# Offsets between the matmul operands in SBUF: the high parts 32 bytes off the weights' line, modulo 512

## The chip, the cores and the metric

The program runs on 1 core of one Trainium2 chip. The metric is the device time of one execution in microseconds (us). Most executions of one kernel agree within 0.3%. A second figure is the span of a profiled execution, from the first to the last instruction in the trace.

## The reference

Two transformer blocks run one after the other on 512 tokens of width 1024, all in float32. What matters here is where the matrix products are:

```python
def first_block(x, ...):
    h = x
    h = h + hybrid_mixer(rms_norm(h, norm1_g), w_in, ..., w_out)
    h = h + sq_relu_mlp(rms_norm(h, norm2_g), w_up, w_down)
    return rms_norm(h, final_norm_g)

def second_block(x, c, ...):
    h = rmsnorm(x, g_norm1) * (1.0 + scale1) + shift1
    proj = h @ w_in
    ...
    merged = (jax.nn.sigmoid(gate_fox) * (y_fox @ w_branch_fox)
              + jax.nn.sigmoid(gate_dsa) * (y_dsa @ w_branch_dsa))
    x = x + gate1 * (merged @ w_out)
    h2 = rmsnorm(x, g_norm2) * (1.0 + scale2) + shift2
    x = x + gate2 * (jnp.square(jax.nn.relu(h2 @ w_mlp1)) @ w_mlp2)
    return rmsnorm(x, g_final)
```

The mixers (a gated convolution and a chunked retention in the first block; forgetting attention and a top-128 sparse attention in the second) stand between the projections. Each MLP has an inner width of 4096.

## The kernel before

**Three products for one.** Every large product is made in fp32r from operands that are split in two. Weights come from HBM into `raw` (512 KB a piece, one of four slots). ScalarE copies a slot to `w_hi` (line 1213), which rounds it, and GpSimd writes the rest, `w_lo = raw - w_hi` (line 542). The activations are split the same way: `u_hi`/`u_lo` hold the output of a norm, `y_hi`/`y_lo` the inner activations of an MLP or the outputs of the attention heads, `m_hi`/`m_lo` the merged branches ahead of the second `w_out`. A product is then the sum of high by high, high by low and low by high, gathered in one PSUM bank.

**The loop that does most of the work** is `unit` (line 581): for each of 8 chunks of the contraction it issues three matmuls of 128x512. The tensor named first in the call is the stationary one (the 128x128 block that is loaded into the array), the second is the moving one (128x512, streamed through):

```python
for k in ks[part[0]:part[1]]:
    c = slice(k * P, k * P + cols)
    for w, r in ((w_hi, r_hi), (w_hi, r_lo), (w_lo, r_hi)):
        last = pe.matmul(ps[0:cols, bank, :], w[:, s, c], r[:, k, :], ...)
```

`r` is `u` in the norm-fed products and the first half of each MLP, `y` in the second half of the first MLP, `m` in the second block's `w_out`. In the profile a matmul is written `ps<-moving,stationary`, so `ps<-u_hi,w_hi` streams `u_hi` past `w_hi`. In some places the roles are turned: `rv_pass` (line 727) and `value_slot` (1008) hold `u` and stream the weights, `down_rows` (1127) and `last_down_rows` (1157) hold `y` and stream the weights in the order (y_hi, w_hi), (y_hi, w_lo), (y_lo, w_hi). `branch` (1071) holds weights and streams `y`.

**The order of the work** is written out by hand in each engine's block; semaphores `raw_ready`, `hi_ready`, `lo_ready`, `used` and `bank_free` hand the four weight slots and the PSUM banks around. While the array streams for one matmul, the stationary block of the next is loaded. Attention work (lines 960 to 987) is laid between pieces of `unit` from about 670 to 840 us.

**Addresses.** A helper `sb(name, shape, dtype)` places tensors one behind the other in each partition; each starts at the next multiple of 32 bytes, and a stack (`where=`) lets later tensors take the place of closed ones. `sb("to_line", [P, 72])` fills up to address 32768, where `xres` starts. From there on `xres`, `u_hi`, `u_lo`, `y_hi`, `y_lo` and `raw`, `w_hi`, `w_lo` follow with 16 KB each, a multiple of 512 bytes, so all of them start at 0 modulo 512. So do `m_hi`, `m_lo`, `q_up`, `q_dn`, `k_both` and `vtoks`, which lie behind them. A chunk of an activation is 2048 bytes wide and a 128-column block of weights 512 bytes, so that every operand of the matmuls above starts at 0 modulo 512.

Of the kernel before, what the change touches and what calls it, by code (L numbers as in the profile page):

```python
# [25 lines left out]
F32R = mybir.dt.float32r  # L26
# [4 lines left out]
P = 128  # L31
T = 512
NT = T // P
D = 1024
KC = D // P
# [9 lines left out]
SLOTS = 4  # L45
# [126 lines left out]
def build(nc, tab, x, norm1_g, w_in, conv_w, conv_norm_g, ret_norm_g, w_out, norm2_g, w_up, w_down,  # L172
# [30 lines left out]
    with ctx:  # L203
        def sb(name, shape, dt=F32, where=ctx):
            return where.enter_context(nc.sbuf_tensor(name, shape, dt))
# [31 lines left out]
        sb("to_line", [P, 72])  # L237

        xres = sb("xres", [P, KC, T])
        u_hi, u_lo = sb("u_hi", [P, KC, T], F32R), sb("u_lo", [P, KC, T], F32R)  # L240
        y_hi = sb("y_hi", [P, KC, T], F32R)
        scores = ExitStack()
        sb("y_lo_front", [P, NQ, T], where=scores)
        work = sb("work", [P, NT - 1, T], where=scores)
# [1 line left out]
        scores.close()  # L246
        y_lo = sb("y_lo", [P, KC, T], F32R)
        raw = sb("raw", [P, SLOTS, KC * P])
        w_hi, w_lo = sb("w_hi", [P, SLOTS, KC * P], F32R), sb("w_lo", [P, SLOTS, KC * P], F32R)

        one = ExitStack()
        fades = sb("fades", [P, P + 4 * NQ], where=one)
# [30 lines left out]
        two = ExitStack()  # L283
        merge = ExitStack()
        vtoks = sb("vtoks", [P, 2, NT, QW], where=merge)
        q_up, q_dn = sb("q_up", [P, 4, T], F32R, where=merge), sb("q_dn", [P, 4, T], F32R, where=merge)
        merge.close()
        m_hi, m_lo = sb("m_hi", [P, KC, T], F32R, where=two), sb("m_lo", [P, KC, T], F32R, where=two)
        keys_done = ExitStack()
        gates = sb("gates", [P, 4, T], where=keys_done)  # L290
        keys_done.close()
# [2169 lines left out]
```

## Time and profile before

| | |
|---|---|
| median of 3 runs | 1351.55 us (1351.45 to 1351.58) |
| the profiled execution's own time | 1352.54 us |
| its span | 1350.7 us |
| PE (matmul) busy | 1339.7 us, 99% of the span |
| weight loads (PEld) busy | 1094.2 us |
| DVE, ACT, POOL busy | 756.1, 525.9, 563.0 us |
| mean granted TensorE clock | 0.998 |

The profiled execution took 1.0 us more than the median of the runs, of which 1.8 us lie outside its span. In the profile a matmul's duration is longer than its share of the array: it begins when its turn starts and its modelled end lies behind the last column's way through the array, so neighbours overlap. What a matmul costs in a stream is the distance from its start to the next start.

### The profile page before, as it was taken

The numbers are of one execution on the slowest core, as the hardware profiler recorded it, in microseconds if no ns is written. First come the engines' busy times: TensorE is split into PE (matmuls) and PEld (weight loads), VectorE is DVE, ScalarE is ACT, GpSimd is POOL, SyncE is SP. The second block draws the span as 40 slices with busy tenths as digits, with TensorE's granted clock in tenths as the row PEclk, the third lists the DMA queues.
The fourth block names the chain that finished last, engine by engine and source line by source line (L and its number), as shares of the span: only waits on it lengthen the run. The fifth ranks groups of instructions, "written<-read, shape, count | busy, mean of one in ns | idle before, by whom it ended". The sixth has DMA issues, their size and how long they took to land.

```text
span 1350.7 us, 18066 instructions
## 1 busy us (share of the span) xinstructions
PE 1339.7 (99%) x6376; PEld 1094.2 (81%) x6380; DVE 756.1 (56%) x1085; ACT 525.9 (39%) x830; POOL 563.0 (42%) x230
## 2 busy tenths in 40 slices
PE   9999999999999999999999999999999999999998
PEld 8888878888888888886877777888878888888887
DVE  4555578475664655877788774434563241432355
ACT  6344234422323224254366665232355133142333
POOL 5334344454553635524222223444434534345351
PEclk9999999999999999999999999999999999999999
DMA  7232245555655645423212323333423423324221
GB/s 230 80 97 78 91 130 171 164 167 177 198 168 163 183 143 166 112 91 95 63 56 86 95 63 94 109 94 105 129 73 100 125 78 109 93 79 123 78 94 63
DMA packets 212807, 155.74 MB, mean 115 GB/s; under 512 B 8932, under 2 KB 193760, under 8 KB 212744
## 3 DMA queue, kind: packets, MB, share of 16 engines
q1 hardware_dynamic: 212280, 154.43, 38.4%
q8 instruction: 39, 0.64, 0.2%
q10 hardware_dynamic: 464, 0.48, 0.1%
q14 instruction: 24, 0.20, 0.0%
HBM read 152.75 MB, written 4.74 MB: 117 GB/s over the span
## 4 chain that ended last, share of the span: by engine, by line
PE 53%; DVE 1%; ACT 1%; issue 0%; POOL 0%; ACTq 0%; DVEq 0%
PE ps L581 28%; PE ps L1127 11%; PE ps L1071 3%; PE ps L1008 3%; PE ps L987 1%; PE ps L974 1%; PE ps L1157 1%; PE ps L960 1%; PE ps L961 1%; PE ps L947 0%; PE ps L964 0%; PE ps L921 0%; PE ps L925 0%; PE ps L922 0%; PE ps L1096 0%
## 5 line engine op out<-in xcount | busy, mean ns | idle before, releaser
L542 POOL TENSOR_TENSOR w_lo<-raw,w_hi 128x1024 fp32r<-128x1024 f32 x222 | 560.0, 2530 | 758.1 <-ACT w_hi L1213 738.0
L581 PE MATMUL ps<-u_hi,w_hi 128*128 128x512 f32 x944 | 378.5, 401 | 0.8 <-POOL w_lo L542 0.5
L581 PE MATMUL ps<-u_hi,w_lo 128*128 128x512 f32 x944 | 368.3, 390 | 0.0
L581 PE MATMUL ps<-u_lo,w_hi 128*128 128x512 f32 x944 | 367.5, 389 | 0.0
L1213 ACT ACTIVATE w_hi<-raw 128x1024 fp32r<-128x1024 f32 x222 | 231.6, 1053 | 289.3 <-PE ps L581 116.8
L581 PEld LDWEIGHTS ps<-u_hi,w_lo 128*128 128x128 f32 x944 | 177.2, 188 | 37.7
L581 PEld LDWEIGHTS ps<-u_hi,w_hi 128*128 128x128 f32 x944 | 178.1, 189 | 36.3 <-issue 1.6
L581 PEld LDWEIGHTS ps<-u_lo,w_hi 128*128 128x128 f32 x944 | 177.6, 188 | 34.9 <-issue 1.0
L581 PE MATMUL ps<-y_hi,w_hi 128*128 128x512 f32 x320 | 125.3, 391 | 0.1
L581 PE MATMUL ps<-y_hi,w_lo 128*128 128x512 f32 x320 | 124.5, 389 | 0.0
L581 PE MATMUL ps<-y_lo,w_hi 128*128 128x512 f32 x320 | 124.5, 389 | 0.0
L1432 ACT ACTIVATE nsq<-ps 128x512 f32<-128x512 f32 x64 | 38.3, 598 | 198.6 <-PE ps L581 193.6
L1127 PE MATMUL ps<-w_hi,y_hi 128*128 128x512 f32 x224 | 87.1, 389 | 0.0
L1127 PE MATMUL ps<-w_lo,y_hi 128*128 128x512 f32 x224 | 87.1, 389 | 0.0
L1127 PE MATMUL ps<-w_hi,y_lo 128*128 128x512 f32 x224 | 87.1, 389 | 0.0
L2000 DVE SCALAR_TENSOR_TENSOR acc<-adaw,vec,acc 128x1536 f32<-128x1536 f32 x28 | 82.5, 2946 | 1.9 <-DVE y_lo L2054 1.5
L2110 DVE TENSOR_TENSOR nt<-nsq 128x512 f32<-128x512 f32 x32 | 27.9, 873 | 98.1 <-ACT nsq L1432 98.0
L2049 DVE TENSOR_TENSOR nt<-nsq 128x512 f32<-128x512 f32 x32 | 24.3, 758 | 84.5 <-ACT nsq L1432 83.9
L581 PEld LDWEIGHTS ps<-y_hi,w_hi 128*128 128x128 f32 x320 | 60.1, 188 | 13.9 <-issue 1.1
L581 PEld LDWEIGHTS ps<-y_lo,w_hi 128*128 128x128 f32 x320 | 60.1, 188 | 12.5 <-issue 0.2
L581 PEld LDWEIGHTS ps<-y_hi,w_lo 128*128 128x128 f32 x320 | 60.1, 188 | 12.6
L2132 DVE SCALAR_TENSOR_TENSOR nt<-ps,rinv,gate_row 128x512 f32<-128x512 f32 x21 | 15.8, 751 | 92.4 <-PE ps L1127 92.4
(317 smaller groups left out, 1878.8 us busy)
## 6 DMA issues: line engine op xcount, KB each, us to landing
raw<-w_in SPq DMA_DIRECT2D x69, 512.0 KB, 3.7
raw<-w_mlp SPq DMA_DIRECT2D x64, 512.0 KB, 3.8
adaw<-w_ada SPq DMA_DIRECT2D x32, 768.0 KB, 4.6
raw<-w_up SPq DMA_DIRECT2D x32, 512.0 KB, 6.1
raw<-w_down SPq DMA_DIRECT2D x32, 512.0 KB, 5.5
raw<-w_out SPq DMA_DIRECT2D x16, 512.0 KB, 4.2
bias_rows<-bias_rows SPq DMA_DIRECT2D x4, 635.0 KB
xtok<-x SPq DMA_DIRECT2D x4, 512.0 KB, 7.3
```

The lines of the kernel that those rows point to most:

```text
L542: pool.tensor_tensor(w_lo[:, s, :], raw[:, s, :], w_hi[:, s, :], ALU.subtract).then_inc(lo_ready[s], 1)
L581: last = pe.matmul(ps[0:cols, bank, :], w[:, s, c], r[:, k, :], start=(k == ks[0] and w is w_hi and r is r_hi), stop=(k == ks[-1] and w is ...
L960: pe.matmul(ps[:, bank, 0:keys], q_up[:, at, q], k_both[:, at, 0:keys], start=True, stop=False)
L1008: last = pe.matmul(ps[:, i, :], u[:, k, t], w[:, s, c], start=(k == 0 and u is u_hi and w is w_hi), stop=(k == KC - 1 and u is u_lo))
L1071: last = pe.matmul(ps[:, b, :], w[:, 2, c], r[:, k, :], start=(k == k0 and w is w_hi and r is y_hi), stop=(k == k0 + NQ - 1 and w is w_lo))
L1127: last = pe.matmul(ps[:, i, :], h[:, k, t], w[:, s, c], start=(k == 0 and h is y_hi and w is w_hi), stop=(k == KC - 1 and h is y_lo))
L1213: act.activation(w_hi[:, s, :], raw[:, s, :], ACT.Copy).then_inc(hi_ready[s], 1)
L1432: act.activation(nsq[:, s % 2, :], ps[:, s, :], ACT.Relu).then_inc(bank_free[s], 1)
L2000: dve.scalar_tensor_tensor(a, adaw[:, b, :], c, a, ALU.mult, ALU.add).then_inc(sem("acc_done"), 1)
L2049: dve.tensor_tensor(nt[:, s % 2, :], nsq[:, s % 2, :], nsq[:, s % 2, :], ALU.mult).then_inc(sem("mlp_sq"), 1)
L2110: dve.tensor_tensor(nt[:, s % 2, :], nsq[:, s % 2, :], nsq[:, s % 2, :], ALU.mult).then_inc(sem("mlp_sq"), 1)
L2132: dve.scalar_tensor_tensor(gated[i], ps[:, i, :], facts[:, i:i + 1], gate_row[:, c], ALU.mult, ALU.mult).then_inc(bank_free[i], 1)
```

## The change

Small fillers are put between the tensors, and three declarations of two tensors are split so that a filler can stand between them. Nothing else is touched: no instruction is added or removed, and the order on every engine stays.

```diff
         xres = sb("xres", [P, KC, T])
-        u_hi, u_lo = sb("u_hi", [P, KC, T], F32R), sb("u_lo", [P, KC, T], F32R)
+        sb("to_line1", [P, 4])
+        u_hi = sb("u_hi", [P, KC, T], F32R)
+        sb("to_line2", [P, 4])
+        u_lo = sb("u_lo", [P, KC, T], F32R)
+        sb("to_line3", [P, 4])
         y_hi = sb("y_hi", [P, KC, T], F32R)
+        sb("to_line4", [P, 118])
...
         raw = sb("raw", [P, SLOTS, KC * P])
-        w_hi, w_lo = sb("w_hi", [P, SLOTS, KC * P], F32R), sb("w_lo", [P, SLOTS, KC * P], F32R)
+        sb("to_line5", [P, 126])
+        w_hi = sb("w_hi", [P, SLOTS, KC * P], F32R)
+        w_lo = sb("w_lo", [P, SLOTS, KC * P], F32R)
+        sb("to_line7", [P, 60])
...
         vtoks = sb("vtoks", [P, 2, NT, QW], where=merge)
+        sb("to_line_q", [P, 8], where=merge)
         q_up, q_dn = sb("q_up", [P, 4, T], F32R, where=merge), sb("q_dn", [P, 4, T], F32R, where=merge)
         merge.close()
-        m_hi, m_lo = sb("m_hi", [P, KC, T], F32R, where=two), sb("m_lo", [P, KC, T], F32R, where=two)
+        m_hi = sb("m_hi", [P, KC, T], F32R, where=two)
+        sb("to_line_m", [P, 8], where=two)
+        m_lo = sb("m_lo", [P, KC, T], F32R, where=two)
```

With every start rounded up to 32 bytes, a filler of 4 numbers (16 bytes) takes 32 bytes, one of 118 takes 480, one of 126 takes 512, one of 60 takes 256 and one of 8 takes 32. The starts modulo 512 become:

| tensor | before | after | after, from `w_hi` |
|---|---|---|---|
| xres | 0 | 0 | -64 |
| u_hi | 0 | 32 | -32 |
| u_lo, y_lo, raw, w_hi, w_lo | 0 | 64 | 0 |
| y_hi | 0 | 96 | +32 |
| m_hi, vtoks | 0 | 320 | +256 |
| m_lo, q_up, q_dn, k_both, probt_even, prob_odds | 0 | 352 | +288 |

`nt`, `nsq`, `small` (the identity), `ones`, `prob_evens` and `probt_odd` lie ahead of `xres` and stay at 128.

## Rows read from the trace of the kernel before

**Rows 1.** The page's head: span, and busy time, share and instructions of PE.

```profile
span 1350.7 us, 18066 instructions
...
PE 1339.7 (99%) x6376; PEld 1094.2 (81%) x6380; DVE 756.1 (56%) x1085; ACT 525.9 (39%) x830; POOL 563.0 (42%) x230
```

**Rows 2.** Who made PE wait: us in total, times, longest us (longest row).

```profile
PE ps L644 <- POOL epsc L537: 1.4, 1, 1.4
```

**Rows 3.** The chain that ended last: start us, us, what, with its count.

```profile
947.02 43.53 PE ps L581 x192
...
1323.21 13.62 PE ps L1157 x60
```

**Rows 4.** Matmul groups of the split products, shapes apart: count | busy us, mean ns.

```profile
L581 PE MATMUL ps<-u_hi,w_hi 128*128 128x512 f32 x944 | 378.5, 401 | 0.8 <-POOL w_lo L542 0.5 <-issue 0.2
...
L581 PE MATMUL ps<-y_hi,w_hi 128*128 128x512 f32 x320 | 125.3, 391 | 0.1
...
L1127 PE MATMUL ps<-w_hi,y_hi 128*128 128x512 f32 x224 | 87.1, 389 | 0.0
...
L1008 PE MATMUL ps<-w_hi,u_hi 128*128 128x512 f32 x64 | 26.4, 413 | 0.0
...
L1071 PE MATMUL ps<-y_hi,w_hi 128*128 128x512 f32 x64 | 24.9, 389 | 0.0
...
L581 PE MATMUL ps<-m_hi,w_hi 128*128 128x512 f32 x64 | 24.9, 389 | 0.0
...
L727 PE MATMUL ps<-w_hi,u_hi 128*128 128x512 f32 x32 | 12.3, 400 | 0.5 <-issue 0.5
...
L1157 PE MATMUL ps<-w_hi,y_hi 128*128 128x512 f32 x28 | 10.9, 389 | 0.0
```

**Rows 5.** Timeline of PE in the first MLP, first and twelfth matmul in a row.

```profile
259.82 0.39 PE L581 MATMUL ps<-u_hi,w_hi 128*128 128x512 f32 x1
...
262.31 0.39 PE L581 MATMUL ps<-u_hi,w_lo 128*128 128x512 f32 x1
```

**Rows 6.** Timeline of the weight loads at the same place.

```profile
260.05 0.19 PEld L581 LDWEIGHTS ps<-u_hi,w_lo 128*128 128x128 f32 x1
260.27 0.19 PEld L581 LDWEIGHTS ps<-u_hi,w_hi 128*128 128x128 f32 x1
```

**Rows 7.** Timeline of PE at the end, 256 columns moving: first and last of 24.

```profile
1342.09 0.28 PE L1157 MATMUL ps<-w_hi,y_hi 128*128 128x256 f32 x1
...
1344.84 0.28 PE L1157 MATMUL ps<-w_hi,y_lo 128*128 128x256 f32 x1
```

**Rows 8.** Window around 620 us: us, busy of five engines, granted clock, DMA share, GB/s.

```profile
619.00:621.50 2.50, 2.50 (x7) 1.92 (x7) 2.31 (x7) 0.64 (x1) 1.78 (x1) 0.50 0.00 0
```

**Rows 9.** Timeline of PE in that window, first and sixth matmul in a row.

```profile
619.13 0.63 PE L1008 MATMUL ps<-w_hi,u_hi 128*128 128x512 f32 x1
...
621.27 0.63 PE L1008 MATMUL ps<-w_hi,u_lo 128*128 128x512 f32 x1
```

**Rows 10.** Timeline of PE after a run of transposes, nine starts in a row (five shown).

```profile
68.14 0.39 PE L581 MATMUL ps<-u_lo,w_hi 128*128 128x512 f32 x1
68.38 0.39 PE L581 MATMUL ps<-u_hi,w_lo 128*128 128x512 f32 x1
...
69.08 0.39 PE L581 MATMUL ps<-u_hi,w_lo 128*128 128x512 f32 x1
69.30 0.39 PE L581 MATMUL ps<-u_hi,w_hi 128*128 128x512 f32 x1
...
70.00 0.38 PE L674 MATMUL ps<-qf,kf 128*128 128x128 f32 x2
```

**Rows 11.** The weight slots' makers, GpSimd and ScalarE, and one DMA issue line.

```profile
L542 POOL TENSOR_TENSOR w_lo<-raw,w_hi 128x1024 fp32r<-128x1024 f32 x222 | 560.0, 2530 | 758.1 <-ACT w_hi L1213 738.0
...
L1213 ACT ACTIVATE w_hi<-raw 128x1024 fp32r<-128x1024 f32 x222 | 231.6, 1053 | 289.3 <-PE ps L581 116.8
...
raw<-w_mlp SPq DMA_DIRECT2D x64, 512.0 KB, 3.8
```

**Rows 12.** Window over the attention stretch, columns as in rows 8.

```profile
640.00:840.00 200.00, 198.66 (x1229) 156.78 (x1233) 149.06 (x404) 116.60 (x257) 54.72 (x23) 1.00 0.29 79
```

## The prediction

> **What bounds the kernel now.** I read the page's head first. PE is busy for 1339.7 of 1350.7 us [rows 1], and the longest of its few waits is 1.4 us [rows 2]: no engine and no DMA holds PE up, so only the length of PE's own stream counts. The mean durations of the groups (389 to 413 ns) [rows 4] are no price, because neighbours overlap. The price is the distance between starts, and the chain of waits gives it best: 192 matmuls of 128x512 in 43.53 us, which is 226.7 ns each [rows 3]. The timeline says the same, 11 distances in 2.49 us, 226.4 ns [rows 5].
>
> At full clock (2.4 GHz) 512 columns at one per cycle would take 213.3 ns. So each of these matmuls carries 13.3 ns, or 32 cycles, that stream nothing. Three views say what kind of thing this is:
> - With 256 columns moving, 23 distances take 2.75 us, 119.6 ns each [rows 7]; 256 columns are 106.7 ns, so the extra is 12.9 ns. It belongs to a matmul (or to its weight load), not to a column.
> - At half clock (granted 0.50, that is 1.2 GHz) [rows 8], five distances take 2.14 us, 428 ns [rows 9]; 512 columns are 426.7 ns. Here the extra is gone. A fixed number of TensorE cycles for changing weights would have shown as 27 ns each, 133 ns over the five. So the extra looks like data that don't come fast enough at full clock, not like work of the array.
> - The load of the next stationary block starts with the stream of the current matmul: loads at 260.05 and 260.27, matmuls every 0.227 from 259.82 [rows 5, 6]. Two reads of SBUF run at once, both from a start at 0 modulo 512.
> - Right behind a run of transposes the same matmuls with the same addresses are uneven: 8 distances in 1.86 us, 232.5 ns in the mean, with steps of 0.24 us (68.14 to 68.38) and of 0.22 us (69.08 to 69.30) [rows 10]. Only their phase in time is different. A toll that each weight load pays in any case would not do this.
>
> I read this as two SBUF reads that get into each other's way by a measure that depends on how they lie to each other. An offset in address is then as good as one in time, and this is what the change touches.
>
> **The change part by part.** It removes and adds no instruction, DMA or wait. Three things move.
>
> (1) What streams against what is loaded. In a triple of `unit` with `u`, the pairs (moving now, loaded for the next) are (u_hi, w_hi), (u_lo, w_lo), (u_hi, next w_hi). After the change their distances modulo 512 are -32, 0, -32 bytes; with `y` moving +32, 0, +32; with `y` held and weights moving (lines 1127, 1157) -32, 0, -32; with `m` 256, 288, 256. So of each triple two are shifted, and all three for `m`. The groups of [rows 4] hold 944 + 320 + 224 + 64 + 64 + 64 + 32 + 28 = 1740 triples, 5220 matmuls. Shifted are 2 x 1676 + 3 x 64 = 3544 of them.
>
> The trace of before has no 128x512 fp32r matmul with a shifted pair, so the price of one is bounded from both sides. Best end: the whole extra goes, 213.3 ns, -13.3 ns each, 3544 x 13.3 = -47.3 us. Worst end: each costs the longest step seen, 0.24 us [rows 10], +13.3 ns, +47.3 us. The nearest row is the one in which only the phase differs [rows 10]. It shows a step of 0.22 us (0.215 to 0.225 at its two decimals) as its shortest, and 232.5 ns as its mean. I take 222 ns, the upper half of the shortest step, because the third matmul of a triple stays as it was and hands its state on to the next. That is -4.67 ns each, 3544 x 4.67 = **-16.5 us**.
>
> A rule speaks against this. The Trainium skill ("SBUF — State Buffer", section on the two separate sides) says that PE never waits on another reader. By it the distance to the loaded block could do nothing and this sum would be zero; the uneven distances and the half-clock row [rows 9, 10] do not fit it well, though it speaks of other engines and not of PE's own two reads. The same skill ("TensorE: Matmul & The Clock Gate", back-to-back issue gap) gives N/2.4 + 2.5 ns, 215.8 ns for 512 columns, so by that page the extra here is 10.9 ns, and an estimate with all of it gone from the shifted ones is -38.5 us; the trace shows 226.7, not 215.8.
>
> (2) The splitters. ScalarE, GpSimd and DVE now read and write tensors at other offsets. `raw`, `w_hi`, `w_lo` keep their distance of 0, so the 2530 and 1053 ns a slot [rows 11] stand. The splits of activations now have 32 bytes between their two sides. Priced at zero: a slot is used by 24 matmuls, 5.44 us, against 2.53 us of GpSimd and 1.05 us of ScalarE, and DMA pieces land 3.8 us after issue [rows 11], with four slots in turn. Even at the best end, 5.12 us a slot, this cover holds. The cover would be gone only with GpSimd at twice its time; then every slot would cost PE what GpSimd takes beyond 5.1 us.
>
> (3) Attention operands. `k_both` and `q` stay at one distance (+288 both), `vtoks` and `probt_even` get 32 bytes apart, and the identity stays at 128 while `prob_odds` goes to 352. These are 128-column pieces among 1229 matmuls in 200 us [rows 12]. I take zero, with +/-1 us for the range. In this stretch DVE is busy 149 of 200 us and PE idle 1.3; DVE is what is late next if PE gets quicker there, and it may keep 1 or 2 us of the gain.
>
> Sum: 1350.7 - 16.5 = 1334.2 us of span, 1336.0 us for an execution like the profiled one (1352.54), and, as its own time stands 1.0 us over the median of the runs, **1335.0 us** against 1351.55.
>
> **The rivals.**
> - A, the forecast: shifted pairs get in each other's way less, but not never. 1335 us; from 1346 (1.5 ns each) to 1317.
> - B, full relief: the shifted pairs run at 213.3 to 216 ns, 3544 x 10.7 to 13.3 = -38 to -47 us, 1304 to 1313 us. For it: the extra is wholly absent at half clock [rows 9]. Against: 0.22 us is the shortest step that any phase has brought [rows 10].
> - C, nothing: the extra is a toll of any weight load at full clock, whatever the addresses (one port taken in turns). 1351.5 us. For it: it is the same 12.9 to 13.3 ns in the steady rows of lines 581 and 1157 [rows 3, 7]. Against: the uneven steps. To this belongs that the change doesn't do what it says, if a filler of 16 bytes were not rounded to 32; the starts listed ahead speak against it.
> - D, slower: the even 226.7 ns is a settled state, which the stream finds when every pair has the same distance. With -32, 0, -32 each matmul hands the next a changed phase and the stream never settles; every shifted matmul then costs the unsettled mean of 232.5 ns [rows 10], +5.8 ns, 3544 x 5.8 = +20.6 us, 1372 us. It decides as soon as the mean of a triple passes 226.7 ns. For it: all unsettled phases but one in [rows 10] cost more than the settled one. Against: the unsettled steps are on both sides of 226.7, so the settled state is not the best.
>
> **How the numbers follow.** A measurement of this kernel can tell about 0.2%, 2.7 us. Chances: A 0.37, B 0.14, C 0.18, D 0.31. So faster 0.51, same 0.18, slower 0.31. The time is that of A, the likeliest. For the range I leave out the lower half of B and the end of D: 1309 to 1371 us. A alone would be 1317 to 1346.
>
> **What would show it.** In the changed kernel the chain's row of 192 matmuls (43.53 us) should read about 42.9 us where `u` or `y` is in play (two of three at 222), and the starts in the first MLP should step by 0.22, 0.23, 0.22. B would give 41.8 us and steps of 0.21 or 0.22; C exactly 43.5; D 44.2 or more, with uneven steps in the MLPs where there are none now. The `m` product tells 256 and 288 apart from 32: if its row changes and the others don't, the distance matters but 32 bytes are too few. Weight loads should keep their 0.19 us and their start with the stream. I am wrong in kind if the steady rows stay at 226.7 ns, or if the time changes through waits on `w_lo`, or in the attention stretch alone.

## The result, and the profile after

The changed kernel takes 1378.01 us (1377.91 to 1379.37, 3 runs) against 1351.55 us, a ratio of 1.0199 (95% interval 1.0176 to 1.0222). It is slower by 26.5 us; 1335 us were forecast, and the range ended at 1371. The spans of the two profiled executions differ by 26.9 us.

The head of the page after, answering to [rows 1]:

```profile
span 1377.6 us, 18066 instructions
...
PE 1366.7 (99%) x6376; PEld 1094.2 (79%) x6380; DVE 757.8 (55%) x1085; ACT 526.1 (38%) x830; POOL 562.6 (41%) x230
```

The chain of waits after (start us, us, what, with its count), answering to [rows 3]. Lines are 11 further on than before: 592, 1138 and 1082 for 581, 1127 and 1071.

```profile
952.75 5.58 PE ps L592 x24
958.33 5.55 PE ps L1082 x24
963.88 44.80 PE ps L592 x192
...
1059.39 44.53 PE ps L1138 x192
1103.91 44.80 PE ps L592 x192
```

PE still works all the time, with the same instructions and the same 1094.2 us of weight loads. Each matmul of 512 columns is only further from the next. What stood at 43.52 us for 192 is now 44.80 where `u` or `m` is streamed (233.3 ns each) and 44.53 where `y` is held (231.9 ns); where `y` is streamed (line 1082) 24 take 5.55 us (231.2 ns), where 24 at the old price are 43.53 / 8 = 5.44 us. The timeline of PE in the first MLP, which was even before [rows 5], shows how (start us, us, engine, line, operation):

```profile
264.84 0.40 PE L592 MATMUL ps<-u_hi,w_lo 128*128 128x512 f32 x1
265.07 0.40 PE L592 MATMUL ps<-u_hi,w_hi 128*128 128x512 f32 x1
265.31 0.39 PE L592 MATMUL ps<-u_lo,w_hi 128*128 128x512 f32 x1
265.54 0.40 PE L592 MATMUL ps<-u_hi,w_lo 128*128 128x512 f32 x1
...
267.64 0.40 PE L592 MATMUL ps<-u_hi,w_lo 128*128 128x512 f32 x1
```

12 distances from 264.84 to 267.64 take 2.80 us, 233.3 ns each. They repeat every three matmuls: at the trace's resolution of 1 ns the steps are 235, 231, 234, over and over. So the stream does settle, in a cycle as long as the triple, and all three pay, the unshifted one (`u_lo` against `w_lo`) too.

The distance alone doesn't set the price. Streamed `u` and held `y` both see -32, 0, -32, and cost 233.3 and 231.9 ns. Streamed `y` and held `u` both see +32, 0, +32 (the prediction gives no distances for held `u`), and cost 231.2 and 233.3 ns (held `u`: 106 distances in a row from 644.8 us).

One place got quicker. The last 24 matmuls, with 256 columns moving, answer to [rows 7] (timeline of PE after, first and last of them):

```profile
1368.97 0.28 PE L1168 MATMUL ps<-w_hi,y_hi 128*128 128x256 f32 x1
...
1371.67 0.28 PE L1168 MATMUL ps<-w_hi,y_lo 128*128 128x256 f32 x1
```

The 23 distances take 2.70 us, 117.6 ns each as summed from the single starts, where they took 2.75 us, 119.6 ns each.

The account closes. Over each trace I summed by how much the start that follows each 128x512 matmul of these products is later than 226.67 ns (distances under 300 ns alone). Before it is 3.0 us, after 29.9 us; the difference is that of the spans, 26.9 us, within 0.1 us. By kind it is 15.4 for streamed `u`, 5.0 for streamed `y`, 4.0 for held `y`, 1.4 for held `u` and 1.3 for `m`. GpSimd's slots (2528 ns now, 2530 before), ScalarE's (1053 ns both) and the waits (the longest 1.4 us, before and after) played no part.

### The profile page after: what moved, and what is told of

Same layout as the page of the kernel before. It is cut to its first block, busy times and chain, and to the rows that moved or that the text cites. A ratio compares the mean times of both kernels' runs of the same rounds, so it can differ in the third digit from the quotient of the medians.

```text
span 1377.6 us, 18066 instructions
## 1 busy us (share of the span) xinstructions
PE 1366.7 (99%) x6376; PEld 1094.2 (79%) x6380; DVE 757.8 (55%) x1085; ACT 526.1 (38%) x830; POOL 562.6 (41%) x230
## 4 chain that ended last, share of the span: by engine, by line
PE 53%; DVE 1%; ACT 1%; issue 0%; POOL 0%; ACTq 0%; DVEq 0%
PE ps L592 28%; PE ps L1138 11%; PE ps L1082 3%; PE ps L1019 2%; PE ps L1168 2%; PE ps L998 1%; PE ps L985 1%; PE ps L971 1%; PE ps L972 1%; PE ps L958 0%; PE ps L932 0%; PE ps L975 0%; PE ps L936 0%; PE ps L933 0%; PE ps L1107 0%
## 5 line engine op out<-in xcount | busy, mean ns | idle before, releaser
L553 POOL TENSOR_TENSOR w_lo<-raw,w_hi 128x1024 fp32r<-128x1024 f32 x222 | 559.6, 2528 | 784.5 <-ACT w_hi L1224 762.1
L592 PE MATMUL ps<-u_hi,w_hi 128*128 128x512 f32 x944 | 384.3, 407 | 0.4 <-POOL w_lo L553 0.4
L592 PE MATMUL ps<-u_hi,w_lo 128*128 128x512 f32 x944 | 374.1, 396 | 0.0
L592 PE MATMUL ps<-u_lo,w_hi 128*128 128x512 f32 x944 | 371.3, 393 | 0.0
L1224 ACT ACTIVATE w_hi<-raw 128x1024 fp32r<-128x1024 f32 x222 | 231.6, 1053 | 297.7 <-PE ps L592 121.6
```

What stands on the lines that cost most here:

```text
L553: pool.tensor_tensor(w_lo[:, s, :], raw[:, s, :], w_hi[:, s, :], ALU.subtract).then_inc(lo_ready[s], 1)
L1224: act.activation(w_hi[:, s, :], raw[:, s, :], ACT.Copy).then_inc(hi_ready[s], 1)
```

## The experiments

Two questions: is it the distance between operands at all, and if so, which distance costs what? Times of a kernel with two runs or more are given with their interval; the prices in ns come from one profiled execution, as (last start - first start) / number of distances, in long runs of one kind. Where only one run is given, it has no interval, and the kernel before, run once beside it, took 1354.49 us, 2.9 us over its median. So a time difference of some 3 us between such runs says nothing by itself; there the prices carry the argument.

**All by 64 bytes.** One filler ahead of `u_hi`; nothing else.

```diff
         xres = sb("xres", [P, KC, T])
-        u_hi, u_lo = sb("u_hi", [P, KC, T], F32R), sb("u_lo", [P, KC, T], F32R)
+        sb("to_u", [P, 16])
+        u_hi = sb("u_hi", [P, KC, T], F32R)
+        u_lo = sb("u_lo", [P, KC, T], F32R)
```

> Everything behind xres lies 64 bytes further on, all distances between matmul operands are 0 again. Distance theory (what counts is how far the moving operand lies from the block that is loaded at the same time): 226.7 ns a matmul everywhere, 1351.5 us. Line theory (what counts is that w_hi and w_lo no longer start at 0 modulo 512, so that each 512-byte block crosses a line): the changed kernel's 231 to 233 ns, about 1378 us.

1351.64 us, ratio 1.0003 (0.9992 to 1.0014). Every long row of the chain of waits of this kernel (start us, us, what, as in all chains below) is as before:

```profile
1039.54 43.52 PE ps L1130 x192
1083.06 43.52 PE ps L584 x192
```

The line theory falls: moving all of them by 64 bytes changes nothing. What is left is how they lie to each other.

**u_hi alone.**

```diff
-        u_hi, u_lo = sb("u_hi", [P, KC, T], F32R), sb("u_lo", [P, KC, T], F32R)
+        u_hi = sb("u_hi", [P, KC, T], F32R)
+        sb("to_ul", [P, 8])
+        u_lo = sb("u_lo", [P, KC, T], F32R)
```

> u_hi alone lies 32 bytes below all the rest, which is at 0 among itself. Distance theory: products with u at 233.3 ns (44.80 us for 192, as in the changed kernel), those with y and m back at 226.7 ns (43.52 us), so about 3100 x 6.6 = 20 us over before, less in the attention stretch: 1366 to 1372 us. Line theory: 1378 us, with y and m slow too.

1368.23 us, ratio 1.0119 (1.0090 to 1.0148), as the distance theory asks. The two kinds stand side by side in the chain of waits of this kernel, held `y` at 43.56 us and streamed `u` at 44.79:

```profile
1051.81 43.56 PE ps L1130 x192
1095.37 44.79 PE ps L584 x192
```

Against the kernel before in the same runs (1351.41 us) that is 16.8 us more, just the 15.4 + 1.4 that the account above gives streamed and held `u`. The other 9.7 of the 26.5 us fit the 10.3 that it gives `y` and `m`.

**Both parts alike.** Here the distances no longer alternate within a triple. This is the test of rival D's mechanism. Fillers of 8, 24, 112 and 32 numbers stand ahead of `u_hi`, `y_hi`, `raw` and the block of `m_hi`, so that `u` lies at 32, `y` at 128, the weights at 64 and `m` at 192 modulo 512.

> Both parts shifted alike: u -32, y +64, m +128 from the weights, so the distances no longer alternate within a triple. Theory of the mix (the stream can't settle because -32, 0, -32 alternate; one distance for all settles again as cheaply as 0): 43.52 us for 192 of u, y and m, about 1351 us. Theory of the distance itself (any distance but 0 gives the two reads more collisions): 230 to 240 ns, 1375 us or more. If collisions need equal places modulo 512, they would vanish: 213 to 216 ns, near 1290 us.

1377.95 us, ratio 1.0191 (1.0161 to 1.0220). The chain of waits of this kernel, with `m`, held `y` and streamed `u` in turn:

```profile
962.09 44.62 PE ps L587 x192
...
1057.44 44.80 PE ps L1133 x192
1102.24 44.79 PE ps L587 x192
```

A constant -32 costs `u` 233.3 ns, just what -32, 0, -32 cost. `m` at +128 costs 232.4 ns and held `y` at -64 233.3. Streamed `y` at +64 costs 228.9 ns in four of its five long runs and 233.3 in the other, 229.8 in the mean: one distance, one kernel, two settled prices. The theory of the mix falls: an even distance of -32 is no cheaper than an alternating one. So does the theory that collisions need equal places, since none of -32, +64, -64 and +128 helps.

**Both parts alike, further off.** The same with `u` at 0, `y` at 224, weights at 128 and `m` at 384.

> As the run with both parts shifted alike, but u -128, y +96, m +256. Mix theory: 226.7 ns for all three, 1351 us. Distance theory: each product gets a price of its own, between 220 and 240 ns, by its distance; the rows of 192 matmuls of u, y and m read them off separately.

1381.06 us, ratio 1.0214 (1.0184 to 1.0244). Streamed `u` at -128 costs 232.4 ns in some long runs and 233.3 in others (233.0 in the mean), streamed `y` at +96 233.3, held `y` at -96 234.2. But `m` at +256, the first row of the chain of waits of this kernel, is as it was:

```profile
966.50 43.56 PE ps L586 x192
...
1060.64 44.96 PE ps L1132 x192
1105.60 44.80 PE ps L586 x192
```

**The rest of the scan.** `u` at 160, `y` at 192, `m` at 224 bytes from the weights.

> Both parts alike: u 160, y 192, m 224 bytes from the weights, the distances not yet seen up to 256 (with their negatives where the roles are turned). If the price repeats every 256 bytes, 160 is -96, 192 is -64 and 224 is -32: 234.3, 233.3 and 233.3 ns, and for the turned roles of y (-192, like +64) 229.8 ns; about 1379 us. Without such a period they are free, and one of them could be below 226.7.

1380.76 us in one run beside 1354.49 for the kernel before. The prices are those of 256 bytes less: `u` at 160 costs 234.3 ns where -96 cost held `y` 234.2, `m` at 224 costs 233.3 as `u` does at -32, held `y` at -192 costs 228.9, the lower of the two prices of +64. Streamed `y` at 192 costs 233.3.

**Low parts apart.** `u` at 256 and 0, `y` at 0 and 32, `m` at 0 and 256 (high, low).

> u: high part 256 bytes off, low part at 0. y: high part at 0, low part 32 bytes off. m: high at 0, low 256 bytes off. If 256 bytes are as good as 0 for each pair by itself, u and m stay at 226.7 ns. If one pair in three at 32 bytes is enough to unsettle the stream (as 256, 288, 256 was for m in the changed kernel, 233.3), y runs at 230 to 233 ns, 1356 us in all; if each pair pays for itself alone, y pays a third, 228.9 ns.

1362.49 us in one run beside 1354.49. The chain of waits of this kernel, held `y`, then streamed `u`:

```profile
1045.32 44.79 PE ps L1135 x192
1090.10 43.53 PE ps L589 x192
```

Distances of 256 and 0 mixed cost `u` nothing, so with the two runs above 256 bytes is the period, as far as these distances show it. One pair in three at 32 bytes costs held `y` all of 233.3 ns and streamed `y` 232.1 in the mean (231.7 in four long runs, 233.3 in one). A pair doesn't pay for itself alone; the whole triple pays.

**Fewer held columns.** Does the toll of 32 cycles that all these matmuls had before come from the loaded block?

```diff
-                    unit(st, s, q * 4 + i, u_hi, u_lo)
+                    unit(st, s, q * 4 + i, u_hi, u_lo, cols=P // 2 if st is st_mlp2 else P)
...
```

> Addresses as before. The stationary blocks are cut: 64 columns in the second MLP's products with u, 32 in the first MLP's products with y, 96 in six of eight units of the second w_out; the rest of each product is left out. The moving operand stays 512 columns. If the 32 extra cycles come from the load of the next block running into the stream, they shrink with what is loaded: 16, 8 and 24 cycles, that is 220.0, 216.7 and 223.3 ns a matmul, 1338 us in all. If they are a fixed toll of each matmul or load, all stay at 226.7 ns and the time at 1351 us.

1357.82 us beside 1354.49, too little between two single runs to tell. The prices tell: 64 held columns cost 230.0 ns, 96 cost 230.0, 32 cost 231.7, none of them less than 226.7. (PE alone, below, gives the same three.) The chain of waits of this kernel, held `y` (untouched), then streamed `u` with 64 held columns:

```profile
1043.71 43.52 PE ps L1127 x192
1087.22 44.16 PE ps L581 x192
```

Neither theory holds. The toll isn't in proportion to what is loaded, and it isn't fixed. I read a shorter load as a change of phase in time, like a shift in address; no run tests that reading.

**Finer distances.** The allocator gives 32 bytes; 4 come from a view into a longer tensor.

```diff
-        u_hi, u_lo = sb("u_hi", [P, KC, T], F32R), sb("u_lo", [P, KC, T], F32R)
+        u_hi = sb("u_hi", [P, KC * T + 8], F32R)[:, 4:4 + KC * T].rearrange("p (k t) -> p k t", k=KC)
...
```

> Distances smaller than the 32 bytes of the allocator, for both parts alike (the low parts another 256 bytes on): u 16, y 8, m 4 bytes. If places inside 32 bytes are one and the same to the two reads, all stay at 226.7 ns, 1351 us. If the price moves smoothly with distance, they lie between 226.7 and 233.3 ns (m nearest to 226.7), near 1365 us. If a few bytes are enough to pass between two reads, one of them is below 226.7 ns.

1375.62 us beside 1354.49. `u` at 16 bytes costs 231.6 ns, `y` at 8 costs 233.3, `m` at 4 costs 237.8, the dearest so far. Turned round, held `u` at -16 costs 233.3 and held `y` at -8 230.7. Nothing is smooth here, and 4 bytes are not too few.

**PE alone.** To scan the distance I left the computation out and let PE work through lines of 36 equal matmuls, with nothing else running (from 30 to 700 us every other engine is busy 0.00 us):

```python
for _ in range(36): pe.matmul(p(), h(0), m(4), start=True, stop=True)
```

`h` is the held block, `m` the moving operand, and the number the byte offset.

> No part of the kernel: the whole computation is left out. PE alone works, with 36 matmuls of one kind per line of code, all operands in SBUF and no other engine busy. The lines go through the distance of the moving operand from the held block, 0 to 252 bytes in steps of 4; then distance 0 with both moved by 32 and 64 bytes; then 96, 64, 32 held columns; then 384, 256, 128 moving columns; then bf16; two PSUM banks in turn; two moving places (0, 32) in turn; two held places in turn; both in turn. Distance theory: distance 0 gives 226.7 ns wherever both lie, -32 and 64 give 233.3 and 229.8 as in the kernel, and the price is a function of the distance alone. If another engine's or the DMAs' traffic is needed for the effect, all distances give the same. If it is the distance from one moving block to the next that counts, every line with one fixed place gives 226.7 and only the lines with two places in turn differ. A distance below 226.7 ns, if there is one, is one to use in the kernel.

The timeline of PE for this kernel (start us, us, engine, line, operation, count), one row a line of code, for distances 0, 4, 8, 20 and 24:

```profile
26.02 8.32 PE L57 MATMUL ps<-moved,held 128*128 128x512 f32 x36
34.18 8.68 PE L58 MATMUL ps<-moved,held 128*128 128x512 f32 x36
42.70 8.55 PE L59 MATMUL ps<-moved,held 128*128 128x512 f32 x36
...
67.67 8.80 PE L62 MATMUL ps<-moved,held 128*128 128x512 f32 x36
76.31 8.57 PE L63 MATMUL ps<-moved,held 128*128 128x512 f32 x36
```

From one start to the next is the price of 36: 8.16 us at 0 (226.7 ns), 8.52 at 4 (236.7), 8.64 at 20 (240.0). The kernel's prices come back within some 1 ns, with no other engine running and a DMA share of 0.00: 32 gives 233.3 ns, 64 228.9, 96, 128 and 192 233.3, 160 234.3, and 224 (that is -32) 233.3. So do those of the finer distances, 231.7 at 16, 233.3 at 8 and 236.7 at 4 where the kernel had 231.6, 233.3 and 237.8. Every one of these lines has one fixed moving place, so steps from one moving block to the next aren't needed for the effect. Of the 64 distances from 0 to 252 seven gave 226.7 ns: 0, 28, 60, 156, 236, 240 and 252. **None gave less.** The dearest, at 240 ns, were 20, 132, 196 and 244. One more line of the same timeline matters here, bf16 operands, with the line behind it for its end:

```profile
659.96 7.72 PE L134 MATMUL ps<-moved,held 128*128 128x512 bf16 x35
667.33 8.56 PE L135 MATMUL ps<-moved,held 128*128 128x512 f32 x36
```

The bf16 starts lie 215.8 ns apart, summed from the single starts. Both tensors moved by 32 or 64 bytes together stay at 226.7 ns. Two PSUM banks in turn change nothing. With 256 columns moving the price at distance 0 is 120.0 ns. Of the lines with places 0 and 32 in turn, only the moving place in turn costs 231.7 ns, only the held place 235.0, and both together 233.3; the last is line 139:

```profile
700.67 8.55 PE L139 MATMUL ps<-moved,held 128*128 128x512 f32 x36
709.07 3.16 PE L140 MATMUL ps<-moved,held 128*128 128x512 f32 x13
```

**PE alone, two pairs.** The lines are pairs that alternate, triples, fewer moving columns, bf16, and six matmuls behind three transposes.

> PE alone again, the computation left out. (1) Own or next: held 32 with moving 0 in turn with held 0 with moving 32. Each matmul's own distance is -32 or +32, but the block that is loaded while it streams lies at distance 0. If the block loaded during the stream counts, 226.7 ns; if a matmul's own block counts, 233.3. The opposite line (held 0 with moving 0, held 20 with moving 20) has own distances 0 and loaded ones 20 and -20: above 230 ns by the first, 226.7 by the second. (2) Triples as in the kernel, distance of the high and of the low part: (0, 0) 226.7; (-32, 0) 233.3 and (32, 0) 231.2 as the changed kernel's u and y; (-32, -32) 233.3; (252, 252), (240, 240), (236, 236), (156, 156), (60, 60), (28, 28) 226.7 each if the one-pair prices hold in triples. (3) The first matmuls run at half clock with distance 32 and 20: 426.7 ns if the price exists only at full clock. (4) 384 and 256 columns at distances 32 and 20: the same cycles over the columns as at 512 (48 and 64) if the price belongs to the load, in proportion if it belongs to the columns. (5) bf16 at ten distances: 215.8 ns at all of them if half the bytes leave room. (6) Three transposes and six matmuls in turn: with distance 0 the six cost 230 to 233 ns each as in the kernel's broken stretches; a distance that costs less there would be worth a kernel.

The timeline of PE for this kernel: the first matmuls, then lines in which two places alternate:

```profile
10.38 1.65 PE L60 MATMUL ps<-moved,held 128*128 128x512 f32 x3 [10.38 <-ACT moved L36]
11.83 1.48 PE L61 MATMUL ps<-moved,held 128*128 128x512 f32 x3
13.11 15.18 PE L62 MATMUL ps<-moved,held 128*128 128x512 f32 x60
28.13 8.44 PE L63 MATMUL ps<-moved,held 128*128 128x512 f32 x36
...
40.05 8.53 PE L65 MATMUL ps<-moved,held 128*128 128x512 f32 x36
48.42 3.79 PE L66 MATMUL ps<-moved,held 128*128 128x512 f32 x16
52.05 8.65 PE L67 MATMUL ps<-moved,held 128*128 128x512 f32 x36
60.54 3.83 PE L68 MATMUL ps<-moved,held 128*128 128x512 f32 x16
```

(1) Line 67 has own distances of 0 and loaded ones of 20 and -20: 8.49 us, 235.8 ns (236.7 once it has settled). A matmul's own distance doesn't explain that. Line 65 has the same four places, paired the other way round: own distances of 20 and -20, loaded ones of 0. It costs 232.5 ns. With 0 and 32 the same exchange gives 233.3 ns where the loaded distances are 32 (line 139 of the run before) and 230.0 where the own ones are (line 63). The steps from one moving place to the next are alike in both pairings, so the block that is loaded meanwhile weighs more than the own. It isn't all of it: lines 63 and 65 have loaded distances of 0 and yet cost more than 226.7. Whether the own distance does that or the steps between places, no line tells apart. (2) Triples give the changed kernel's prices to 0.1 ns: (-32, 0) 233.3, (32, 0) 231.1, (-32, -32) 233.3. (252, 252), (156, 156), (60, 60) and (28, 28) give 226.7, but (240, 240) gives 236.7 and (236, 236) 228.9. (3) In line 61, from 11.83 to 13.11, three matmuls at the dear distance of 20 take 427 ns each, just 512 columns at 1.2 GHz, and the matmuls at distance 0 behind them take 427 too: at half clock the distance costs nothing. (The clock's view shows 1.00 for this short stretch; I take half clock from the starts, which are 427 ns apart like those in [rows 9].) (4) 384 columns cost 416 cycles at 32 and 252 and 427 at 20; 256 columns cost 280 at 32 and 252 and 293 at 20. So with 256 columns 32 bytes are cheaper than 0 (288), as at the end of the changed kernel. (5) bf16 keeps its 215.8 ns at 13 of 14 distances and takes 216.7 at 2 bytes. (6) Three transposes and six matmuls take 1.72 us at 0, 1.70 to 1.71 at 236 and 252, 1.75 at 20.

**PE alone, five entries.** Is the price a matter of the distance, or also of what went before?

> PE alone, the computation left out. Each of the distances 0, 252, 240, 236, 156, 60, 28 and 32 bytes is run for 36 matmuls in a row, five times, each time behind something else: seven matmuls at distance 20, eight at 32, three transposes, three bf16 matmuls, three with 256 columns. If a distance has one price, the five settled values of each agree (226.7 for all but 32). If the stream can settle in more than one state, those that gave two values so far (252 with 226.7 and 230.5; 240 with 226.7 and 236.7; 236 with 226.7 and 228.9) do so again, by what went before; the theory that 0 is the safe one asks for 226.7 ns from all five entries at distance 0.

Settled, 0, 252, 156, 60 and 28 gave 226.7 ns from each of the five entries, 236 gave 228.9 and 32 gave 233.3. 240 gave 236.7 four times and 233.3 once (behind bf16). The scan had found 226.7 at 236 and 240 both. So a distance can have more than one settled price. For 240 it goes by what ran before.

**u 4 bytes below.** Of the cheap distances behind transposes, 252 bytes is tried in the kernel.

> Both parts of u lie 4 bytes below the weights (modulo 256), all else at distance 0. By the price list of the PE-alone kernels, for a settled stream: products that stream u cost 226.7 ns as before; those that hold u and stream weights see +4 bytes, 236.7 ns, about 270 matmuls, +2.7 us; in the pieces behind transposes six matmuls in a row cost 15 ns less than at distance 0, with some 110 such pieces -1.6 us. In all 1352 to 1353 us, no difference that can be told. If the price list doesn't carry over from PE alone to the kernel, the streamed u would show it: 230 ns or more, 1360 us or more.

1361.18 us, ratio 1.0070 (1.0053 to 1.0086): slower, where no difference was expected. Streamed `u` costs 230.6 ns (44.27 us for 192), though the same triple cost 226.7 on PE alone; `y` beside it is untouched. Held `u`, which sees +4, costs 233.2, not the 236.7 of PE alone. The chain of waits of this kernel, held `y`, then streamed `u`:

```profile
1046.47 43.53 PE ps L1129 x192
1090.00 44.27 PE ps L583 x192
```

The price list carries over for the multiples of 32, and for 16 and 8 bytes, that both tried, but not here. Which difference between the two (the moving blocks step by 2048 bytes in the kernel, and the tensors lie further apart) picks the other settled state, I didn't try.

## Why the prediction was wrong

**The bound was read rightly.** PE's stream alone sets the time, and what moved is the distance between starts, in all groups that were named, by as much as the spans differ. The reading that two reads get in each other's way held for what comes on top of 226.7 ns: that answers to address with all else still, and at half clock it is gone. For the 13.3 ns below, which every 512-column fp32r stream has at full clock, no run shows it.

**The step that failed is the price of a shifted matmul in part (1).** I took 222 ns, below the settled 226.7, from the shortest single step of an unsettled stretch [rows 10]. The measured price is 231.2 to 233.3. A single step of 0.22 us was never a price: in that stretch it stood between steps of 0.24, and what an unsettled stretch costs is its mean. That mean, 232.5 ns, stood in the same rows and came within 1.3 ns. In part that is luck: it is the price of an unsettled stream at distance 0, and what was to be priced is a settled stream at another distance. I also had the wrong picture of 226.7 as a half-bad value with room below it. The scan shows it as the floor for 512 columns: none of 64 distances is under it. No long run of 512-column matmuls in the trace of before had shown a mean under 226.7 at full clock either, and that should have moved the forecast to the side of a loss.

**A second term was too small:** the count. I let the unshifted matmul of a triple stay at its price. It pays like the others (235, 231, 234), so 5220 matmuls count and not 3544. With the chain's prices: streamed and held `u` 3120 x 6.7, streamed `y` 1152 x 4.6, held `y` 756 x 5.2, `m` 192 x 6.7, 31.4 us in all. That is 4.5 us over the 26.9 found. 3.0 of it was paid before already, in stretches that were unsettled.

**Rival D** forecast 1372 us against 1378. Its price came near, but by the luck told above, as its mechanism was wrong. An even distance of -32 costs as much as an alternating one, and the stream does settle, only in a dearer cycle. Its 20.6 us falls short of the 26.9 by the count, which was too small by a third; 5.8 ns on all 5220 would be 30.3, less what the stretches that were unsettled before already paid.

**Rival C** (nothing, whatever the addresses) falls by the result and by the run with `u_hi` alone, 1368.23 us; only the 13.3 ns at distance 0 may still be such a toll. The rule that PE never waits on another reader (the Trainium skill, "SBUF — State Buffer", on the two separate sides) can't be stretched to PE's own two reads: the place of one to the other alone took `u` from 226.7 to 233.3 ns. **Rival B** falls by the scan. The 215.8 ns of the Trainium skill ("TensorE: Matmul & The Clock Gate", back-to-back issue gap) are right for bf16, where the trace gives 215.8 ns; for fp32r the floor seen here is 226.7.

**Parts (2) and (3)** held, as far as the account shows: the splitters' slots take what they took, and the starts of the split products' matmuls make up the 26.9 us to 0.1, so that all the rest, the attention stretch with it, comes to nothing in sum. No run changes either part by itself. The sign for `m` was told too: 256, 288, 256 costs 233.3 ns, 256 alone nothing, so there the 288 of the low part did it.

**Open:** what the 32 cycles over 512 columns are, and why they go away at half clock; they don't shrink with a shorter load. Also why 256 columns are cheaper at 32 bytes than at 0, why the same three distances cost `u` and `y` different amounts, and what picks one of several settled states, which were seen at 4, 236, 240 and 252 bytes and in the kernel at +64 and -128. No version that beats the kernel before was found.

## What to carry to other kernels

In a dense stream of fp32r matmuls with 512 columns moving, keep the moving operands, high and low parts alike, at a distance of 0 modulo 256 bytes from the held blocks; fillers that broke this cost this PE-bound kernel 0.7 to 2.1%. With 256 columns moving, 32 bytes were cheaper (116.7 against 120.0 ns). Check it by the distance between starts in the timeline or in the chain (226.7 ns for 512 columns at full clock), not by mean durations or busy shares, which hardly show it (`u_hi` against `w_hi` went from 401 to 407 ns, PE's share stayed at 99%). And when a trace shows a range of steps for one instruction, price a change by their mean, and ask whether anything in the trace is ever better than the settled value before forecasting a gain.

## What the runs showed of the hardware

- A 128x512 fp32r matmul in a stream costs 226.7 to 240.0 ns at full clock, by where its moving operand lies to the block that is loaded meanwhile, modulo 256 bytes, in steps as small as 4 bytes. At half clock it is 427 ns at distance 20 and at 0.
- The block loaded for the next matmul weighs more than a matmul's own: 233.3 against 230.0 ns with places 0 and 32, 235.8 against 232.5 with 0 and 20.
- With 256 columns moving, 32 bytes are cheaper than 0: 116.7 against 120.0 ns on PE alone, 117.6 against 119.6 in the kernel.
- The stream settles in cycles of one to several matmuls, and some distances have more than one such state (240 bytes: 226.7, 233.3 and 236.7 ns). On PE alone at distance 0 the first six steps behind three transposes are uneven, and the first ten behind bf16.
- Fewer held columns make it dearer (230.0 ns with 64, 231.7 with 32, for 226.7 with 128).
- bf16 streams cost 215.8 ns at 13 of 14 distances and 216.7 at the other.
